# Rope rotation in two float32r passes, first projections over eight PSUM banks, and early high parts in a latent-attention layer

## The reference

```python
c_q = rms_norm(u[..., :Q_RANK], q_norm)                  # 384 wide
q = jnp.einsum("bsc,chd->bshd", c_q, w_uq)               # per head 128 plain + 64 rope columns
q_nope, q_rope = q[..., :128], apply_rope(q[..., 128:], cos, sin)
# apply_rope(x): x1, x2 = halves of x;  [x1 * cos - x2 * sin, x2 * cos + x1 * sin]
s = (q_nope @ k_nope.T + q_rope @ k_rope.T) * 192 ** -0.5    # causal mask, then softmax
o = p @ v                                                # 8 heads of 128
y = (o * silu(gate)) @ w_out                             # 1024 x 1024
out = rms_norm(x + y, final_norm)
```

## Time and profile before

| what | value |
|---|---|
| device time, median of 3 runs | 2646.66 us (2645.43 to 2649.67) |
| device time of the profiled execution | 2644.31 us |
| its span, from first to last instruction | 2642.2 us |
| mean granted TensorE clock | 0.99 of full speed |
| projections of the attention layer and attention | about 2212 to 2532 us of the span |
| output projection and final norm | about 2532 to 2642 us |

### The profile page before, as it was taken

The page is one execution under the profiler, slowest core; times in us unless marked ns, Lnnn a source line. Parts: engine busy times, 40 slices in busy tenths (PEclk is TensorE's granted clock), DMA queues, the critical chain, the costliest instruction groups (busy, mean ns, idle before and its releaser), DMA issues.

```text
span 2642.2 us, 32837 instructions
## 1 busy us (share of the span) xinstructions
PE 2555.2 (97%) x12732; PEld 2127.0 (81%) x12732; DVE 1494.2 (57%) x1820; ACT 905.6 (34%) x1265; POOL 1074.3 (41%) x770
## 2 busy tenths in 40 slices
PE   7999999899999989999999999999999999999997
PEld 6888887787788778888888887788888787888876
DVE  4485633376655687677652254667774524555554
ACT  5244235322222343333330032345641422444432
POOL 3453522211233478888854343333355332111111
PEclk9999999999999999999999999999999999999999
DMA  3101021111252122222252122311132311000022
GB/s 132 48 25 41 33 80 40 48 37 45 99 190 70 40 74 86 80 88 80 88 183 96 63 65 72 107 40 44 43 119 80 114 64 30 20 20 17 25 81 78
DMA packets 52888, 184.01 MB, mean 70 GB/s; under 512 B 5409, under 2 KB 9761, under 8 KB 51361
## 3 DMA queue, kind: packets, MB, share of 16 engines
q1 hardware_dynamic: 46560, 147.08, 16.6%
q10 hardware_dynamic: 6208, 35.27, 3.5%
HBM read 149.83 MB, written 32.51 MB: 69 GB/s over the span
## 4 chain that ended last, share of the span: by engine, by line
PE 53%; DVE 6%; ACT 3%; issue 2%; POOL 0%; ACTq 0%; DVEq 0%; POOLq 0%
PE ps L784 10%; PE ps L786 10%; PE ps L785 10%; PE ps L1097 5%; PE ps L1099 5%; PE ps L1098 5%; PE ps L1277 2%; PE ps L1267 1%; PE ps L1195 1%; PE ps L1197 1%; PE ps L1196 1%; DVE tmp L2412 1%; PE ps L1256 0%; PE ps L1255 0%; PE ps L1254 0%
## 5 line engine op out<-in xcount | busy, mean ns | idle before, releaser
L584 POOL TENSOR_TENSOR derived_vectors<-w_staged 1x1 f32<-1x1 f32 x162 | 39.0, 241 | 1398.1 <-PE ps L786 683.9
L587 POOL TENSOR_TENSOR w_low<-w_staged,w_high 128x1024 fp32r<-128x1024 f32 x162 | 433.9, 2678 | 13.0
L848 PE MATMUL ps<-h_mix_high,w_high 128*128 128x512 f32 x688 | 279.6, 406 | 4.6 <-DVE z_hgrn_f L1913 4.6
L850 PE MATMUL ps<-h_mix_high,w_low 128*128 128x512 f32 x688 | 270.4, 393 | 0.0
L849 PE MATMUL ps<-h_mix_low,w_high 128*128 128x512 f32 x688 | 269.8, 392 | 0.0
L585 POOL CAST w_high<-w_staged 128x1024 fp32r<-128x1024 f32 x162 | 167.6, 1035 | 0.0
L848 PEld LDWEIGHTS ps<-h_mix_high,w_high 128*128 128x128 f32 x688 | 130.6, 190 | 30.8 <-issue 5.8
L850 PEld LDWEIGHTS ps<-h_mix_high,w_low 128*128 128x128 f32 x688 | 130.2, 189 | 28.3
L849 PEld LDWEIGHTS ps<-h_mix_low,w_high 128*128 128x128 f32 x688 | 130.7, 190 | 25.3
L784 PE MATMUL ps<-act_high,w_high 128*128 128x512 f32 x352 | 137.1, 390 | 0.7 <-DVE act_low L1850 0.7
L785 PE MATMUL ps<-act_low,w_high 128*128 128x512 f32 x352 | 137.0, 389 | 0.0
(11 more groups left out here) (511 smaller groups left out, 6927.6 us busy)
## 6 DMA issues: line engine op xcount, KB each, us to landing
w_staged<-weights_in SPq DMA_DIRECT2D x178, 512.0 KB, 3.5
w_staged_late<-weights_in SPq DMA_DIRECT2D x22, 512.0 KB, 4.3
gates_loaded<-gates ACTq DMA_DIRECT2D x8, 1024.0 KB, 6.5
gates<-tmp SPq DMA_DIRECT2D x16, 512.0 KB, 2.6
act_raw<-gates SPq DMA_DIRECT2D x16, 512.0 KB, 7.4
gates<-gates_staged_late SPq DMA_DIRECT2D x22, 256.0 KB, 2.0
x_in<-xT_in SPq DMA_DIRECT2D x8, 512.0 KB, 8.1
x_mid<-xT_in ACTq DMA_DIRECT2D x1, 4096.0 KB, 13.3
```

The lines of the kernel that those rows point to most:

```text
L587: nc.gpsimd.tensor_tensor(w_low[:, j], w_staged[:, j], f32(w_high[:, j]), ALU.subtract).then_inc(s_split, 1)
L848: nc.tensor.matmul(ps[:, bank], wH, h1H[:, c, tok], start=(c == 0), stop=False)
L850: done = nc.tensor.matmul(ps[:, bank], wL, h1H[:, c, tok], start=False, stop=(c == DC - 1))
```

## The change

There are three edits. First, q_rope is split into `q_rope_high` (by ScalarE, from the copy that VectorE has made in SBUF) and `q_rope_low` (by VectorE), and the rotation is two float32r matmuls with `rope_rotate_r`, a float32r copy of the matrix, instead of one float32 matmul. VectorE raises `s_pread` after the low part instead of after the copy. Second, the first twelve projections go round all eight banks instead of four, with waits on the earlier users of banks 4 to 7. Third, ScalarE makes the high parts of heads 0 to 6 as soon as the scores are all made and 56 gatings are done, ahead of the load of `x_last`; VectorE makes the low parts of heads 0 and 1 ahead of the last gating; and TensorE's wait for all 64 gatings goes.

```diff
@@ -328,6 +328,8 @@
         rotated = at("q_rope_rotated", [P, S], R(3, 28))
         k_ropeH, k_ropeL = full("k_rope_high", 3, F32R, 16, 1), full("k_rope_low", 3, F32R, 20, 1)
         q_rope = at("q_rope", [P, S], R(3, 24))
+        rope_high, rope_low = at("q_rope_high", [P, S], R(1, 24), F32R), at("q_rope_low", [P, S], R(3, 28), F32R)
+        rotate_r = at("rope_rotate_r", [P, P], R(1, 29), F32R)
         probs_c = at("probs_mla", [P, 2, S], MISC + 4096)
         probsT_c = at("probs_mla_T", [P, 2, S], MISC + 12288)
         y7H, y7L = full("y_mla_high", 2, F32R), full("y_mla_low", 1, F32R)
@@ -401,6 +403,7 @@
         result_sum = Continued(s_hw, 8)
         act_stored, pair_loaded = Continued(s_hm, 16), [s_load, s_gin]
         block_raw, block_high, block_low, corner_term = Continued(s_hst, 14), Continued(s_h2, 16), Continued(s_hout, 8), Continued(s_iTe, 8)
+        rope_highed, rope_copied = Continued(s_bln, 16), Continued(s_bn, 8)
         squares_lowered, latent_added = Continued(s_ha, 12), Continued(s_hscan, 2)
         s_out, s_fin = sem("out_stored"), sem("out_ready")
         s_fsq, s_fsum = sem("last_squares"), sem("last_square_sum")
@@ -758,7 +761,7 @@
             return ps[:, b:b + 2].rearrange("p b n -> p (b n)")[:, 0:mla.items[n][2] * P]
 
         def mla_bank(m):
-            return m % 4 if m < 12 else 7
+            return m % 8 if m < 12 else 7
 
         def mla_done(m):
 
@@ -1204,8 +1207,12 @@
                 if m < 4:
                     t = 6 + m // 2
                     pe.wait_ge(s_free[m], use_of("cgate", 0, 6 + (bank_of("cgate", 0, 0) // 2 + m // 2) % 2) + 1)
+                elif m < 6:
+                    pe.wait_ge(s_crstd, 4)
+                elif m < 8:
+                    pe.wait_ge(s_kr, 2)
                 elif m < 12:
-                    pe.wait_ge(s_pread, m - 3)
+                    pe.wait_ge(s_pread, m - 7)
                 else:
                     pe.wait_ge(s_pread, m)
                 if i in (0, 1):
@@ -1218,7 +1225,8 @@
                 elif i in (3, 5):
                     h = i // 2 - 1
                     pe.wait_ge(s_pread, 16 * p + h + 1)
-                    nc.tensor.matmul(ps[:, bank], rotate[:], q_rope[:, half_of(h)], start=True, stop=True).then_inc(s_rotq, 1)
+                    nc.tensor.matmul(ps[:, bank], rotate_r[:], rope_high[:, half_of(h)], start=True, stop=False)
+                    nc.tensor.matmul(ps[:, bank], rotate_r[:], rope_low[:, half_of(h)], start=False, stop=True).then_inc(s_rotq, 1)
                 elif i in (6, 7, 14, 15):
                     t, h = (0, i - 6) if i < 12 else (1, i - 14)
                     pe.wait_ge(s_split, u0 + 3)
@@ -1294,7 +1302,6 @@
                 if fillers:
                     mla_projection(fillers[-1])
                 mla_values(n)
-            pe.wait_ge(mla.outL, 64)
 
             def last_sum(h):
                 pe.wait_ge(s_fsum, h + 1)
@@ -1764,6 +1771,7 @@
             act.wait_ge(s_cwl, 5)
             act.wait_ge(s_cconst, 32)
             act.dma_start(cos_sin[:], a["cos_sin"]).then_inc(s_cconst, 16)
+            nc.scalar.activation(rotate_r[:], rotate[:], ACT.Copy)
             nc.scalar.activation(causal_r[:], causal[:], ACT.Copy).then_inc(s_ldone, 1)
 
             def mla_gate(i, j):
@@ -1778,6 +1786,12 @@
 
                 p, i = m // 16, m % 16
                 t = i // 12
+                if i in (0, 1):
+                    act.wait_ge(*rope_copied.at(2 * p + i + 1))
+                    act.wait_ge(s_krL, 1)
+                    await_at_least(act, s_rotq, 2 * p)
+                    nc.scalar.activation(rope_high[:, half_of(i)], q_rope[:, half_of(i)], ACT.Copy).then_inc(rope_highed.semaphore, 1)
+                    return
                 if i in (2, 4, 12, 13):
                     h, dst = (i // 2 - 1 if i < 12 else i - 12), q_nopeH
                 elif i in (6, 7, 14, 15):
@@ -1830,10 +1844,13 @@
                     mla_high(fillers[-1])
                 if n + 2 < 64:
                     mla_normed(n + 2)
+            act.wait_ge(mla.scored, 64)
+            act.wait_ge(mla.outL, 56)
+            for m in range(DC - 1):
+                nc.scalar.activation(y7H[:, m], cgate[:, m], ACT.Copy).then_inc(s_y7h, 1)
             act.wait_ge(mla.outL, 64)
             act.dma_start(x5[:], a["x_spill_mla"]).then_inc(s_xld5, 16)
-            for m in range(DC):
-                nc.scalar.activation(y7H[:, m], cgate[:, m], ACT.Copy).then_inc(s_y7h, 1)
+            nc.scalar.activation(y7H[:, DC - 1], cgate[:, DC - 1], ACT.Copy).then_inc(s_y7h, 1)
             split_x(6, x5, None, 0, updated("wob"), late=4, n=DC - 1)
             act.wait_ge(s_l, 52 + 6)
             for h in range(2):
@@ -2555,7 +2572,11 @@
                 t, bank = i // 12, ps[:, mla_bank(m)]
                 if i in (0, 1):
                     dve.wait_ge(s_mm, mla_done(m))
-                    nc.vector.tensor_copy(q_rope[:, half_of(i)], bank).then_inc(s_pread, 1)
+                    nc.vector.tensor_copy(q_rope[:, half_of(i)], bank).then_inc(rope_copied.semaphore, 1)
+                    dve.wait_ge(*rope_copied.at(2 * p + i + 1))
+                    dve.wait_ge(*rope_highed.at(2 * p + i + 1))
+                    await_at_least(dve, s_qready, 2 * p)
+                    low_of(rope_low[:, half_of(i)], q_rope[:, half_of(i)], rope_high[:, half_of(i)]).then_inc(s_pread, 1)
                 elif i in (3, 5):
                     h = i // 2 - 1
                     x, turned = q_rope[:, half_of(h)], rotated[:, half_of(h)]
@@ -2597,6 +2618,10 @@
                 dve.wait_ge(mla.transposed, m + 1)
                 await_at_least(dve, mla.summed, m - 1)
                 nc.vector.tensor_copy(mla.probsT[:, m % 2, 0:nk * P], transposed_flat[:, 0:nk * P]).then_inc(mla.copied, 1)
+
+            def y_low_of(m):
+                dve.wait_ge(s_y7h, m + 1)
+                low_of(y7L[:, m], cgate[:, m], y7H[:, m]).then_inc(s_y7l, 1)
 
             def mla_gated(m):
                 H, j, _ = mla.items[m]
@@ -2626,12 +2651,14 @@
                     mla_max(n + 2)
                 if fillers:
                     mla_read(fillers[-1])
+                if n == 63:
+                    y_low_of(0)
+                    y_low_of(1)
                 mla_gated(n)
                 if n + 2 < 64:
                     mla_inverse(n + 2)
-            for m in range(DC):
-                dve.wait_ge(s_y7h, m + 1)
-                low_of(y7L[:, m], cgate[:, m], y7H[:, m]).then_inc(s_y7l, 1)
+            for m in range(2, DC):
+                y_low_of(m)
             dve.wait_ge(s_xld5, 16)
             split_x(6, x5, None, None, 0, add_to("wob", x5), late=4, n=DC - 1)
             dve.wait_ge(s_l, 52 + 7)
```

## The result

| what | before | after |
|---|---|---|
| device time, median of 7 runs each | 2648.64 us (2645.25 to 2649.67) | 2659.01 us (2655.95 to 2661.41) |
| ratio after to before, 95% interval | | 1.0044 (1.0034 to 1.0053) |
| profiled execution: time, span | 2644.31, 2642.2 us | 2661.41, 2659.6 us |
| mean granted clock | 0.990 | 0.986 |

What follows compares the result with a forecast made beforehand. TensorE, at work for 97% of the span, was taken as the bound. First stretch +2.6, loop +1.2 and boundary -4.9 summed to -1.1: a median of 2645.6 us, range 2641.5 to 2656.

Steps and rivals of the forecast that it cites:

- the lean at the tie: Loop, at 2285.82: VectorE's subtraction and GpSimd's w_low start 0.01 apart; near a coin toss, leaning to VectorE first.
- the hand-over back from ScalarE to VectorE: Loop, between ScalarE's q_rope_high and VectorE's subtraction: takes 0.03, within 2.08 from copy start to bank release.
- The rival's condition: Loop: GpSimd goes first if the subtraction claims some 0.04 after w_low, because ScalarE's copy has three waits.
- an operation printed at 905.58: A traced operation overlapping the one before it, so its true claim came later than printed; used to favour VectorE first.
- the rival: Loop: GpSimd goes first, hole before projection 18 is 2.8 instead of 0.6; +5.5, median 2652, up to 2658; chance 0.32.
- my +0.4: Loop, per head pair: new hole of 0.6 before projection 18 less 0.2 given back by the rotations; three pairs make +1.2.
- the range, 2656: Whole kernel: upper end of the 8-in-10 range 2641.5 to 2656, set to include GpSimd going first with some clock falls.
- The first stretch, +2.6: First twelve projections: scores start 1.9 later and a clock fall adds 0.7; +2.6, bounds +1.0 and +3.5.
- my lower bound: First twelve projections: +1.0 if there is no collision and no fall of the clock.
- The rope edit's gain: Loop rotations: 0.46 instead of 0.86, 0.8 per pair, of which 0.2 is given back (bounds 0 and 0.8).
- The boundary, -4.9: Ahead of the output projection: TensorE starts 2.4 earlier, twelve matmuls at full clock save 2.4 more; bounds -2.4 and -5.
- a hole shorter than 1.85 costs no clock: Ahead of the output projection: the hole shrinks to 0.9, under the 1.85 that cost no clock, so matmuls go at 0.23.

Runs made afterwards that it cites:

- from_bank: Changed kernel with the q_rope_low subtraction taking its first input from the PSUM bank instead of the SBUF copy; 2643.06 us, ratio 0.9986.
- four_banks: Changed kernel without the second edit, so the first twelve projections use four banks as before; 2658.39 us, ratio 1.0043.
- gap_widened: Changed kernel with six long fulfilled waits on GpSimd ahead of w_low of the value unit in the loop's three head pairs; ratio 1.0043.
- gpsimd_second: Changed kernel with one more wait: in the loop's three head pairs, GpSimd's w_low waits for the q_rope_low subtraction of projection 17; 2645.38 us, ratio 0.9993.
- cos_in_loop: Kernel before with the third edit and, in the loop alone, q_rope high part, low part and cosine product from the bank, two float32r rotations; 2642.74 us, ratio 0.9977.
- hole_only: Kernel before with one more wait: in the loop's three head pairs, TensorE's projection 18 (and 34, 50) waits for GpSimd's w_low; 2659.24 us, ratio 1.0046.
- cos_from_bank: Changed kernel with q_rope's high part, low part and cosine product taken from the PSUM bank, replacing the copy and later product; 2643.81 us, ratio 0.9987.
- gpsimd_nudged: Changed kernel with a one-element GpSimd addition right before w_low of the value unit in the loop's three head pairs; ratio 1.0046.
- gpsimd_copy_ahead: Changed kernel with a one-element GpSimd copy right before w_low of the value unit in the loop's three head pairs; ratio 1.005.

## Why the prediction was wrong, point by point

**What failed: the lean at the tie.** I reckoned the subtraction at +1.39 behind the start of the copy and `w_low` at +1.38, and leaned to VectorE going first. The step that failed is the hand-over back from ScalarE to VectorE, which I put at 0.03. Between ScalarE's `q_rope_high` and `q_rope_low` it is 0.09 (2292.83 + 0.63 to 2293.55), so VectorE comes at +1.44, 0.06 late, and the loop costs 14.7 where I had 1.2. The row that I took the 0.03 from was `k_rope_low`, behind one wait; `q_rope_low` stands behind three. Whether their number makes the difference no run shows. The rival's condition, that the subtraction claims "some 0.04 after w_low does", was met in all three pairs. The argument that an operation printed at 905.58 had really claimed later favoured VectorE and was beside the point. A tie that both chains reach from one and the same matmul isn't a coin toss in each pair: in the trace after it falls the same way all three times, by 0.06 or 0.07.

**What the rival had right, and what it missed.** A hole of 2.8 (2.61), the subtraction at 2.9 (2.82) with `w_low` at 2.40 (2.34), an end 0.55 behind it (0.54), 1 to 2 us more by the clock (1.8): all this came. Per pair that is 2.2 + 1.8 on my +0.4, or 4.4; measured +4.05 and +3.88, but +6.79 in the third pair. The 2.9 on top of that, the second fall of the clock behind TensorE's old wait for `k_nope_low`, was in no sum of mine, though it came in all six traces with the hole. I had also put the clock's cost outside the rival's price (its median was 2652, "up to 2658" with the clock), and the range, 2656, cut it off.

**The base.** I counted from 2646.66, the median of three executions; that of seven is 2648.64. Of the 13.4 us between 2645.6 and 2659.01, 2.0 come from there. As a difference, I forecast -1.1 and at most +9.3, and +10.4 came.

**The first stretch, +2.6, was mis-sized.** The idle is 3.50 as reckoned. from_bank, without collision and fall, shows +1.0, as my lower bound had it; the collision adds 0.7 to the idle (3.50 against 2.80). The clock then costs 1.0 to 2.2 (stretches of 25.88 to 27.03 in the traces with eight banks and this idle), and not the 0.7 that I had left over after what eight banks hide. They hide 0.1, by four_banks against gap_widened. Measured +3.70, 0.2 over the bound of +3.5.

**The rope edit's gain.** A pair of 0.46 instead of 0.86 is there, and the loop without the long hole comes out at +0.3 a pair (gpsimd_second 0.29, from_bank 0.34) where I had +0.4: a hole of 0.5 instead of 0.6, and 0.1 to 0.2 given back. I had 0.2 given back, and for the right reason; TensorE's 0.50 for `k_nope_low` is still there in the kernel after.

**The boundary, -4.9,** was right: -4.99, hole 0.74 for 0.9, clock 1.00, and no wait of TensorE for `x_last`. VectorE's first output tile did wait 6.8 for the load; it cost nothing that TensorE's waits show. The argument that a hole shorter than 1.85 costs no clock held there, but not always: behind the same hole cos_in_loop lost 1.6.

## What to carry to other kernels

When an edit puts a VectorE operation with two SBUF inputs on the path, look for what GpSimd does at that moment, and whether one event releases both chains. If so, don't bet on hundredths: take one input from PSUM (0.69 beside a running `w_low`), or order the two with a wait. Price a new hole of over 2 us with the clock behind it, here 1.3 to 1.8 for nine wide matmuls where it fell, inside the case and not beside it, and ask which old wait further on may then bring a second fall. A faster matmul gave back only 0.1 to 0.2 of its 0.8 a pair here, since behind it TensorE waits for VectorE's next low part.

## What the runs showed of the hardware that was not expected

- The length of an idle doesn't by itself say whether the clock falls. 2.15 three times in hole_only: 0.50, 0.50 and 1.00 behind it; 2.61 ahead of projection 18: 0.50 in the kernel after, 1.00 in the first pair of gap_widened; 2.80 at the start of from_bank: 1.00; 2.76 at the start of cos_from_bank: 0.50; 0.74 at the boundary: 1.00 in the kernel after, 0.50 in cos_in_loop. That an idle of 1.85 left the clock at 1.00, on which my prediction leaned, was a reading of one place and no rule.
- A wait that was harmless before may bring the clock down after a change elsewhere. TensorE's wait of 2.1 for `k_nope_low` left the clock at 1.00 in all three pairs of the kernel before, and the clock stood at 0.50 behind it in the third pair of all six traces with the long hole. What decides it stays open: hole_only had its holes of 2.15 and no such fall, cos_from_bank had the fall in two pairs without a long hole.
- VectorE's subtraction with two SBUF inputs wasn't let in between two GpSimd operations that follow each other at once (2.96 and 2.94 in gpsimd_nudged and gpsimd_copy_ahead), even behind a one-element copy.
- Six fulfilled waits on GpSimd between `w_high` and `w_low` moved `w_low` by nothing (+1.38 both times), while putting the wait that ends last behind the fulfilled ones made the hand-over 0.13 longer over two engines (1.44 to 1.57).
